# Gate and up projection of a hybrid decoder step: another order of the feed-forward epilogue on VectorE and ScalarE

## Reference

```python
def swiglu_ffn(h, w_gate_up, w_down):
    gate, up = jnp.split(h @ w_gate_up, 2, axis=-1)
    return (jax.nn.silu(gate) * up) @ w_down
...
x = x + swiglu_ffn(rms_norm(x, norm_ffn[i]), w_gate_up[i], w_down[i])
```

## The kernel before

| j | ACT | DVE |
|---|---|---|
| 0 | `split_hi`, then `silu` of the gate (line 656) | `split_lo`, then `scaled`: gate times rstd (two instructions, line 2163), up times rstd (two, line 2166) |
| 1 | `split_hi`, then `hidden_hi`: rounds the product to `a_hi` (line 660) | `split_lo`, then `hidden`: silu(gate) x up to `f_h` (line 2173) |
| 2 | `split_hi` | `split_lo`, then `hidden_lo`: `a_lo = f_h - a_hi` (line 2177) |

## Time and profile before

### The profile page before, as it was taken

How to read it: one execution, slowest core, us unless ns; L and a number is a source line. 1 busy time by engine, 2 the same in 40 slices (tenths; PEclk the granted TensorE clock), 3 DMA queues, 4 the chain that set the end, 5 groups by cost and what they waited for, 6 DMA issues and landing times.

```text
span 3190.0 us, 72148 instructions
## 1 busy us (share of the span) xinstructions
PE 3064.4 (96%) x27160; PEld 2942.1 (92%) x27160; DVE 1780.2 (56%) x2806; ACT 1387.1 (43%) x2024; POOL 175.7 (6%) x267
## 2 busy tenths in 40 slices
PE   5899999999999999999999999999999999999998
PEld 3899999999998899999999999998899999999997
DVE  2577677677677455455445444556555544554444
ACT  3445445445445344433333333555443333333333
POOL 0112112112111000000000000000000000000000
PEclk8999999999999999999999999999999999999999
DMA  7545545545545455555555555553355555555553
GB/s 209 153 140 158 150 139 156 152 138 156 152 138 156 139 185 179 171 171 166 173 171 172 173 180 166 190 179 121 112 178 170 172 169 172 168 172 175 179 175 130
DMA packets 514690, 519.08 MB, mean 163 GB/s; under 512 B 30875, under 2 KB 437540, under 8 KB 513892
## 3 DMA queue, kind: packets, MB, share of 16 engines
q1 hardware_dynamic: 505490, 498.85, 50.7%
q0 software_dynamic: 2128, 13.69, 1.3%
q10 hardware_dynamic: 6866, 3.50, 0.4%
HBM read 491.99 MB, written 32.82 MB: 165 GB/s over the span
## 4 chain that ended last, share of the span: by engine, by line
PE 85%; DVE 8%; issue 3%; ACT 3%; DMA 1%; ACTq 0%; SPq 0%; DVEq 0%
PE bank L447 26%; PE bank L448 24%; PE bank L449 24%; PE bank L1636 4%; DVE w_lo L435 2%; ACT w_hi L428 2%; DVE f_h L2173 1%; DVE s_dec L2096 1%; PE bank L1774 1%; PE bank L1821 0%; PE bank L1663 0%; DMA hcol<-in_dt_bias_dram 0%; PE bank L980 0%; PE bank L524 0%; DVE qk_sq L1949 0%
## 5 line engine op out<-in xcount | busy, mean ns | idle before, releaser
L435 DVE TENSOR_TENSOR w_lo<-w_raw,w_hi 128x1024 fp32r<-128x1024 f32 x858 | 1049.4, 1223 | 1050.6 <-ACT w_hi L428 1046.7
L428 ACT ACTIVATE w_hi<-w_raw 128x1024 fp32r<-128x1024 f32 x858 | 906.7, 1057 | 1293.0 <-PE bank L449 1283.9
L447 PE MATMUL bank<-h_hi,w_hi 128*128 128x264 f32 x4624 | 1373.4, 297 | 49.7 <-DVE w_lo L435 49.7
L448 PE MATMUL bank<-h_lo,w_hi 128*128 128x264 f32 x4624 | 1317.4, 285 | 0.0
L449 PE MATMUL bank<-h_hi,w_lo 128*128 128x264 f32 x4624 | 1316.9, 285 | 0.0
L447 PEld LDWEIGHTS bank<-h_hi,w_hi 128*128 128x128 f32 x4624 | 875.4, 189 | 92.1 <-DVE w_lo L435 49.3
L448 PEld LDWEIGHTS bank<-h_lo,w_hi 128*128 128x128 f32 x4624 | 877.3, 190 | 1.7
L449 PEld LDWEIGHTS bank<-h_hi,w_lo 128*128 128x128 f32 x4624 | 875.1, 189 | 0.0
L447 PE MATMUL bank<-a_hi,w_hi 128*128 128x264 f32 x1408 | 402.1, 286 | 5.8 <-DVE w_lo L435 3.8
L448 PE MATMUL bank<-a_lo,w_hi 128*128 128x264 f32 x1408 | 402.6, 286 | 0.0
L449 PE MATMUL bank<-a_hi,w_lo 128*128 128x264 f32 x1408 | 401.8, 285 | 0.0
(11 more groups left out here) (357 smaller groups left out, 2848.0 us busy)
## 6 DMA issues: line engine op xcount, KB each, us to landing
w_raw<-in_w_gate_up_dram SPq DMA_DIRECT2D x704, 256.0 KB, 2.9
w_raw<-in_w_in_a_dram SPq DMA_DIRECT2D x388, 256.0 KB, 3.0
w_raw<-in_w_down_dram SPq DMA_DIRECT2D x352, 256.0 KB, 3.0
w_raw<-in_w_out_a_dram SPq DMA_DIRECT2D x128, 256.0 KB, 3.0
w_raw<-in_w_q_b_dram SPq DMA_DIRECT2D x64, 256.0 KB, 3.1
w_raw<-in_w_o_b_dram SPq DMA_DIRECT2D x64, 256.0 KB, 2.9
s_dec<-in_state_delta_dram SPq DMA_DIRECT2D x30, 512.0 KB, 5.3
out_dram<-s_dec SPq DMA_DIRECT2D x28, 512.0 KB, 4.9
```

The source lines that it names most:

```text
L428: nc.scalar.activation(w_hi[:, s % SPL, :], w_raw[:, s, :], ACT.Copy).then_inc(hi_ready, 1)
L435: ops.tensor_tensor(w_lo[:, s % SPL, :], w_raw[:, s, :], w_hi[:, s % SPL, :].bitcast(F32), ALU.subtract).then_inc(lo_ready, 1)
L447: nc.tensor.matmul(bank[bk][:, 0:T], wh, xh, start=first, stop=False)
L448: nc.tensor.matmul(bank[bk][:, 0:T], wh, xl, start=False, stop=False)
```

## The change

The scaling on DVE is taken apart into `scaled_gate` and `scaled_up`. At j = 0 (and 8) DVE's order becomes: gate scaling, `split_lo`, up scaling. On ACT `hidden_hi` moves from j = 1 (9) to j = 2 (10), behind that chunk's `split_hi`. DVE takes the low part at j = 2 as it did. The same is done in the written-out first pass and in the down projection's first chunks. In the first pass DVE's wait for `norm_rstd` moves along, ahead of the gate scaling. The number of instructions and of waits is the same on every engine.

```diff
@@ columns on ACT
-                    elif k in (1, 3) and j == 1:
+                    elif k in (1, 3) and j == 2:
                         hidden_hi(k // 2, FT // 2 - 1)
@@ ffn on ACT
-                        elif j == 1:
+                        elif j == 2:
                             hidden_hi(l, 2 * i - 1)
                         elif j == per:
                             silu(l, 2 * i)
-                        elif j == per + 1:
+                        elif j == per + 2:
                             hidden_hi(l, 2 * i)
@@ add_columns on DVE
+                    if k in (1, 3) and j == 0:
+                        scaled_gate(k // 2, FT // 2 - 1, 1)
                     if not (last and j == 4 * per - 1):
                         split_lo(dve, chunk(base, RAW, 0, j + 1))
                     if k in (1, 3) and j == 0:
-                        scaled(k // 2, FT // 2 - 1, 1)
+                        scaled_up(1)
@@ the helpers on DVE
-            def scaled(l, n, u):
+            def scaled_gate(l, n, u):
                 dve.wait_ge(w_used, UNIT["gu"] * n + (C_GU[l] + UNIT["gu"]))
                 for t in range(2):
                     m = tt(f_gate[:, t, :], bank[4 * u + t][:, 0:T], rstd[:, :], ALU.mult)
                 m.then_inc(gate_scaled, 1)
+
+            def scaled_up(u):
                 for t in range(2):
                     m = tt(f_up[:, t, :], bank[4 * u + 2 + t][:, 0:T], rstd[:, :], ALU.mult)
                 m.then_inc(u_read, 1)
@@ ffn on DVE
                     for j in range(2 * per):
+                        if j == 0 and not first:
+                            scaled_gate(l, 2 * i - 1, 1)
+                        elif j == per:
+                            if first:
+                                dve.wait_ge(norm_rstd, 2 * l + 2)
+                            scaled_gate(l, 2 * i, 0)
                         split_lo(dve, chunk(C_GU[l], 2 * per, i, j + 1))
                         if first and j < 3:
                             unit_dve(dve, 2 * l, 3, j)
                         elif j == 0:
-                            scaled(l, 2 * i - 1, 1)
+                            scaled_up(1)
...
                         elif j == per:
-                            if first:
-                                dve.wait_ge(norm_rstd, 2 * l + 2)
-                            scaled(l, 2 * i, 0)
+                            scaled_up(0)
```

## The result

The changed kernel takes 3136.2 us (median of four runs, 3132.76 to 3140.35) against 3188.7 us of the kernel before (four runs, the three listed above and 3193.02). The ratio is 0.984, 95% interval 0.981 to 0.986. Four further runs of the changed kernel gave 3135.9 us and 0.984 (0.982 to 0.986). The prediction was 3131 us; the difference of the medians is 52.5 us where 53.6 were worked out.

A forecast was written before the change was run, and what follows sets the result against it. PE bounds the kernel, pausing twice a unit in gate and up because ACT waits for DVE. Removing the pauses saves 49.6 + 4.0 = 53.6 us from the median 3184.33, giving 3131 us; range 3121 to 3150 us.

The forecast's parts named there:

- The two pauses and what makes them: Gate and up: ACT's waits for the scaled gate and f_h delay w_hi, then w_lo; PE loses 1.28 us a unit.
- Gate scaling at no cost: Gate scaling ahead of w_lo runs beside ACT's w_hi rounding and ends before w_lo starts; cost 0, upper bound 0.49 us.
- a serial scaling: Rival, 5%: gate scaling and w_hi don't overlap, so 44 x 0.49 = 21.6 us stay; 3152 us.
- a visible return: Rival, 10%: DVE's loop return delays gate scaling and w_lo in half the loop's epilogues; up to 9.8 us, 3140.5 us.
- Silu with the table load: First epilogue of a layer: w_hi, table load and silu take 2.99 us against 2.92, 0.07 late, inside the slack.
- The product and the rounding: DVE multiplies at j = 1; ACT rounds a_hi at j = 2 behind w_hi without a wait; the second pause goes.
- The sum: Forty epilogues in the loops at 1.24 us, 49.6, plus four outside at 1.01, 4.0: 53.6 us saved.
- The terms outside: The four epilogues outside the loops, first and last of each layer, save 1.01 us each, 4.0 us in all.
- all others the same: Sign in the profile after: gate and up stages 50 to 55 us shorter together, every other stage unchanged.
- The loop's return with a fetch: Rival, 2%: each of 20 DVE or ACT loop returns stops to load code, up to 5.7 us each; 3245 us.

The follow-up runs named there:

- silu later: Kernel before with DVE's order kept; ACT does silu in the second chunk and the rounding in the third, each behind that chunk's w_hi: 3134.7 us.
- the gate order alone: Against the kernel before, only the gate scaling goes ahead of w_lo; ACT still rounds the product in the second chunk: 3157.1 us.

## Why the prediction was right

*The two pauses and what makes them* held. Taking away either wait of ACT takes away one pause, and taking both away by other means (silu later) gives the same time as the change.

*Gate scaling at no cost* held. In the loops it starts with the `w_hi` beside it, ends before it, and `w_lo` comes 0.12 us behind `w_hi` at the loop's start and 0.03 us in the other units, as before. The rounding beside it still takes 1.06 us and the pair 0.77. The rivals of a serial scaling and of a visible return are out: no unit in the loops is longer than 23.38 us.

*Silu with the table load* was taken as 0.07 us late. The row at the first epilogue shows less:

```profile
1282.69 1.06 ACT L428 ACTIVATE w_hi<-w_raw 128x1024 fp32r<-128x1024 f32 x1 [1.85 <-PE bank L449]
1283.77 1.28 ACT L656 ACT_TABLE_LOAD   x1
1285.07 0.65 ACT L656 ACTIVATE f_gate<-f_gate 128x528 f32<-128x528 f32 x1
1285.62 1.06 ACT L428 ACTIVATE w_hi<-w_raw 128x1024 fp32r<-128x1024 f32 x1
```

2.93 us from `w_hi` to `w_hi`, since the next activation starts 0.1 us before the one ahead has ended.

*The product and the rounding* held: `a_hi` at 1546.60 waits for nothing, and 1.0 us of idle time of DVE stands before the next `w_lo`.

*The sum* was 53.6 us and is 52.5 by the medians. Of the 5.5 us between 3131 and 3136.2 only 1.1 lie in the sum; the other 4.4 are the median of the kernel before, 3184.33 us by three runs and 3188.7 by four. The term a little too large is 1.24 us for a unit in the loops: 24.577 - 23.373 = 1.20, because eight chunks with an epilogue take 23.37 us, not 8 x 2.917 = 23.34. The terms outside were 1.01 each and are 24.44 - 23.30 = 1.14 for the first of a layer and 12.74 - 11.70 = 1.04 for the last: 40 x 1.20 + 2 x 1.14 + 2 x 1.04 = 52.4. That the medians differ by 52.5 as well is partly luck: the runs of the changed kernel scatter over 8.9 us and those of the kernel before over 12.

*Two things were off without touching the sum.* I split a pause into lateness less 0.27 us of slack plus 0.11 us for the restart; for a pause that stands alone the runs show lateness less 0.19 to 0.25 us, restart included, so that 0.64 was forecast for the gate order alone and 0.53 came. And "all others the same" failed: the down and attention stages differ by -3.7, -5.1 and +0.4 us, of which -1.04 in each down stage is the change's own. That is why the profiled executions differ by 3191.76 - 3133.76 = 58.0 us and the medians by 52.5. I had named this noise for the down stages alone, at 2.9 us for each place; the largest of the three differences lies in the attention stage, which I had not named.

*The loop's return with a fetch* was the rival on the other side. On DVE and ACT it does not occur: the gate scaling starts with the `w_hi` beside it at the loop's start as in the middle. On PE it does, in the down projections: in all 18 returns PE goes on 1.7 us after a packet of code has landed.

The Trainium skill, page "Runtime: NRT & Kernel Launch", section on instruction fetch mechanics, gives PE room for 2048 instructions: PE's loop in gate and up has 16 x 48 = 768 matmuls and weight loads and returns without a pause, the one in the down projection 44 x 48 = 2112 and pauses. The traces agree with the rule, but with only these two sizes they do not show where the limit lies.

## What to carry to other kernels

In a queue that feeds the engine that sets the time, no wait for another engine may stand ahead of the feeding work unless it is satisfied when the queue gets there. Look for it as a row whose idle time names the partner engine, followed by a feeding instruction later than its period. There are two cures, earlier work on the partner or a later place for the waiting instruction, and here they were worth the same (3136 and 3135 us). The step of the feeding instruction, less the chunk time and the slack, estimates the price before anything is built; where two pauses neighbour each other, the second has no slack to spend.

## What the runs showed of the hardware

**A slack pays once.** Alone a late `w_lo` costs 0.53 us, two cost 1.09 with three chunks between them, but 1.20 on neighbouring chunks.

**A loop's return can stop PE for a load of code.** PE's loop of 2112 matmuls and weight loads pauses 1.9 to 2.9 us at each of 18 returns, until 1.7 us after a packet of code has landed. Its loop of 768 returns without a pause in the changed kernel, and the code of both passes written out, 4224 matmuls and weight loads in a row, runs without a pause.

**The clock falls behind some pauses of 2 to 3 us and not behind others.** Nine profiles keep PE's loop in the down projections, so 18 returns, each with a pause of 1.9 to 2.9 us after more than 100 us of dense work; behind 11 of them the granted clock was near 0.5 in the windows of 2 us, and behind 7 it stayed at 1. The length doesn't tell which: it fell behind one of 1.86 us and stayed up behind one of 2.84 us. In the two kernels without the loop it never fell there. It also never fell in the gate and up stages, where the kernel before pauses 0.5 to 0.7 us twice in each 24.6 us. The runs of the changed kernel spread over 8.9 us with the loop and over 2.4 us without it, so most of its scatter seems to go with these pauses. The kernel before without the loop still spreads over 4.9 us in ten runs.
